# Attention on one core: half of each product with V moved between the next scores and the transposes, and output evictions moved behind maxima and exponentials

## The reference, cut to what matters

```
s = q @ k.T                       # 128 x L scores, L = 256, 512, 640 or 768
p = softmax(s)                    # with exp(sink) in the sum in win0 and win1
out = p @ v                       # 128 x 64
```

## Time and profile before

| | |
|---|---|
| median of 3 runs | 2659.6 us (2650.29 to 2662.57) |
| the profiled execution | 2654.18 us, of which the span of its records is 2652.4 us |
| granted TensorE clock over the span | 0.965 of full speed |
| attention `even` | from about 306 to 518 us of the span |
| attention `win0` | from about 2149 to 2247 us |
| attention `win1` | from about 2499 to 2578 us |

### The profile page before, as it was taken

The page is one execution under the profiler, slowest core; times in us unless marked ns, Lnnn a source line. Parts: engine busy times, 40 slices in busy tenths (PEclk is TensorE's granted clock), DMA queues, the critical chain, the costliest instruction groups (busy, mean ns, idle before and its releaser), DMA issues.

```text
span 2652.4 us, 33704 instructions
## 1 busy us (share of the span) xinstructions
PE 2459.0 (93%) x13758; PEld 1967.3 (74%) x13758; DVE 1545.1 (58%) x2428; ACT 947.9 (36%) x1699; POOL 190.3 (7%) x149
## 2 busy tenths in 40 slices
PE   4998898989999999989998889999989989989997
PEld 2875565678888888868886767877768866858765
DVE  4256578638757576665426578878753256363464
ACT  3355556523222121234233332322344135343352
POOL 0000001002101011100000011101100000000010
PEclk8999899999999999999999999999989989999899
DMA  6233200022332332211120144454321120112301
GB/s 233 80 120 114 84 1 1 9 87 88 100 115 98 118 109 95 99 56 64 64 80 1 43 141 157 164 168 145 127 64 59 63 75 1 48 40 86 109 1 64
DMA packets 65994, 223.61 MB, mean 84 GB/s; under 512 B 7216, under 2 KB 10928, under 8 KB 65072
## 3 DMA queue, kind: packets, MB, share of 16 engines
q1 hardware_dynamic: 63648, 214.65, 24.0%
q10 hardware_dynamic: 2192, 6.82, 0.7%
HBM read 219.34 MB, written 2.10 MB: 83 GB/s over the span
## 4 chain that ended last, share of the span: by engine, by line
PE 82%; DVE 9%; ACT 4%; DMA 3%; POOL 1%; issue 1%; SPq 0%; ACTq 0%; DVEq 0%
PE pair L1084 21%; PE pair L1085 20%; PE pair L1086 20%; PE pair L1251 5%; PE side L1300 3%; PE pair L1287 2%; DMA RAW<-in_w 2%; DVE T L1950 2%; ACT T L1697 1%; PE side L1287 1%; PE pair L1110 1%; DVE ACC L1939 1%; DVE WL L1799 1%; PE pair L763 1%; PE pair L1262 1%
## 5 line engine op out<-in xcount | busy, mean ns | idle before, releaser
L1084 PE MATMUL pair<-HH,WH 128*128 128x512 f32 (+1 forms) x2496 | 887.3, 355 | 44.6 <-DVE HL L1958 36.5
L1085 PE MATMUL pair<-HL,WH 128*128 128x512 f32 (+1 forms) x2496 | 872.7, 350 | 0.0
L1086 PE MATMUL pair<-HH,WL 128*128 128x512 f32 (+1 forms) x2496 | 871.9, 349 | 0.0
L1799 DVE TENSOR_TENSOR WL<-RAW,WH 128x1024 fp32r<-128x1024 f32 (+4 forms) x286 | 314.2, 1099 | 524.3 <-ACT WH L1399 513.8
L1399 ACT CAST WH<-RAW 128x1024 fp32r<-128x1024 f32 (+4 forms) x286 | 271.4, 949 | 889.3 <-DMA RAW<-in_w 887.0
L1084 PEld LDWEIGHTS pair<-HH,WH 128*128 128x128 f32 x2496 | 478.7, 192 | 129.7 <-DVE HL L1958 48.5
L1086 PEld LDWEIGHTS pair<-HH,WL 128*128 128x128 f32 x2496 | 479.4, 192 | 59.8
L1085 PEld LDWEIGHTS pair<-HL,WH 128*128 128x128 f32 x2496 | 480.5, 192 | 58.3 <-issue 1.2
L1939 DVE SCALAR_TENSOR_TENSOR ACC<-MODW,CVF,ACC 128x512 f32<-128x512 f32 x336 | 305.5, 967 | 0.0
L1084 PE MATMUL pair<-DH,WH 128*128 128x512 f32 (+1 forms) x624 | 227.9, 365 | 11.8 <-POOL DL L2311 10.4
L1085 PE MATMUL pair<-DL,WH 128*128 128x512 f32 (+1 forms) x624 | 220.8, 354 | 0.0
(11 more groups left out here) (317 smaller groups left out, 2563.7 us busy)
## 6 DMA issues: line engine op xcount, KB each, us to landing
RAW<-in_w SPq DMA_DIRECT2D x250, 512.0 KB, 3.5
MODW<-in_w SPq DMA_DIRECT2D x96, 512.0 KB, 4.3
RAW<-in_w SPq DMA_DIRECT2D x48, 384.0 KB, 3.0
RAW<-in_w SPq DMA_DIRECT2D x16, 256.0 KB, 2.6
DFL<-in_dft_lat ACTq DMA_DIRECT2D x4, 1024.0 KB, 7.2
X<-in_x SPq DMA_DIRECT2D x1, 3072.0 KB, 15.9
out_x<-X SPq DMA_DIRECT2D x8, 256.0 KB, 2.0
RAW<-in_w SPq DMA_DIRECT2D x8, 192.0 KB, 2.4
```

The costliest lines, as they stand in the source:

```text
L1084: mm(out[0:j.m, c:e], wh[k], a, start=k == 0, stop=False)
L1085: mm(out[0:j.m, c:e], wh[k], b, start=False, stop=False)
L1086: ins = mm(out[0:j.m, c:e], wl[k], a, start=False, stop=k == j.k - 1)
L1799: TT(WL[:, j.n % NRING, 0:c], RAW[:, j.n % NRING, 0:c], WH[:, j.n % NRING, 0:c].bitcast(F32), ALU.subtract).then_inc(*dve.mark("lo", j.n))
```

## The change

In PE's loop the half product `pv` no longer follows `turn(u)`. In iteration u it stands between `scores(u+1)` and `turn(u)`, and its index is one less (half u-3 in place of half u-2). The three halves that are left after the loop are computed there. In ACT's loop the output of a block stands behind the exponentials of the next pair and no longer ahead of the first eviction; in DVE's loop it stands behind the two maxima of the next pair.

```diff
@@ PE @@
                 for u in range(n):
                     if u + 1 < n:
                         scores(u + 1)
+                    if u >= 3:
+                        pv((u - 3) // 2, (u - 3) % 2)
                     turn(u)
-                    if u >= 2:
-                        pv(u // 2 - 1, u % 2)
-                for half in range(2):
-                    pv(n // 2 - 1, half)
+                for i in range(n - 3, n):
+                    pv(i // 2, i % 2)
@@ ACT @@
                 for u in range(n):
-                    if u >= 4 and u % 2 == 0:
-                        out(u // 2 - 2)
                     evict(u, 0, 0)
                     if u + 1 < n:
                         exps(u + 1, 0)
                         exps(u + 1, 1)
+                    if u >= 4 and u % 2 == 0:
+                        out(u // 2 - 2)
                     evict(u, 1, 0)
                     evict(u, 1, 1)
```

## The result

The changed kernel takes 2729.54 us (median of 4 runs, 2726.03 to 2734.86), the kernel before 2654.94 us over the same comparison: a ratio of 1.0273 (95% interval 1.0253 to 1.0294), slower by 74.6 us. The profiled execution took 2732.15 us. (In experiment 9 one execution of six was disturbed as a whole, 4138.74 us at a granted clock of 0.555; its ratio and the median given there leave it out.)

The account below looks back on a forecast made before the run. PE, 100% busy in 768-key GQA, and a chain through the other engines both took 4.57 us a pair. Terms 16.3 + 1.2 + 3.3 + 10.7 + 16.5 + 12.7 = 60.7 us gave 2714.9 or 2720.3, forecast 2717, range 2695 to 2742.

Parts of the forecast that it names:

- The half product comes into the chain at full length: 768-key GQA pairs: the 1.44 us half delays the exponentials, 5.93 us a pair against 4.57, 16.3 us over 12 pairs.
- MLA: First layer's MLA attention: 3.05 us more for six rounds, 21 rounds touched, 10.7 us in all, bounds 6 and 21.
- GQA's small pairs: The 8 GQA pairs of 256 keys: between 0 and 6.7 us more, half taken, 3.3 us.
- The three rounds behind them: Three earlier 768-key GQA pairs that meet a small half: 4.97 us a pair, 0.40 more each, 1.2 us.
- The windows: Halves of one, two and three tiles in `win0` and `win1`: 16.5 us more in the first, 12.7 in the second.
- The clock: GQA stretch with PE busy 77%: no loss, since a row at 76% showed a granted clock of 1.00.
- rival 3: Attention rounds with idle PE lose full clock: up to 2857 us, mild form at window starts 2737; chance 0.06 above 80 more.
- my signs of being wrong: Profile after: an exponential before its round's first eviction, 4.6 us spacing in GQA, or a 0.5 clock in these stretches.
- The outputs: Outputs behind ACT's exponentials and DVE's maxima: nothing or some 0.2 us every second GQA pair, at most 2 us, hidden.
- PE's waits within the transposes: Transposes' waits for evictions (10.4 and 10.3 us) and scaling (4.9): given no gain, bound 25.6 us gained.

Follow-up runs that it names:

- experiment 9: The changed kernel run again without edits, for a second profile and a comparison on the same chip: 2727.1 us, 1.0278.
- experiment 4: Against the changed kernel, ACT's first eviction of each pair moved between the two exponentials of the next pair: 2683.25 us, 1.0096 to the kernel before.
- experiment 5: Against the kernel before, the half product put between the first group of transposes and the other three, outputs as before: 2650.19 us, 0.9983.
- filled kernel: The changed kernel with the fourth transpose group of GQA and window pairs written four, five or ten times: 2723.51 us, 1.0259; run again 2722.09 us, 1.0237.
- experiment 1: Against the changed kernel, the outputs on ACT and DVE put back in their old places, PE's order as changed: 2761.2 us, 1.0387 to the kernel before.
- experiment 2: Against the kernel before, only the outputs moved on ACT and DVE, PE's order as before: 2703.5 us, 1.0166.
- experiment 3: Against the kernel before, the whole change in the first layer's attention only, the windows in the old order: 2698.17 us, 1.0146.
- experiment 6: Against the kernel before, the half product put between the third and fourth groups of transposes: 2648.86 us, 0.9973.

## Why the prediction was right, point by point

- *The half product comes into the chain at full length.* Right, to the hundredth where the chain is regular: 5.92 for 5.93 forecast in 12 rounds, which are 16.2 us for 16.3; 6.02 for 4.58 + 1.44 in the windows. With 0.96 for two tiles I had 5.54 and the profiles show 5.59, so a half of two tiles is 1.0. Experiments 4 and 5 show it from two sides: free the first exponential of the eviction and 46 us come back, of which part may be clock; put the half product behind the first group and nothing of the cost is left (0.9983, against 1.0387 with the outputs in the same places).
- *MLA.* 12.8 for 10.7. The rounds with a large half cost 0.77 (0.79 forecast), those with a small one 0.55 where I had scaled 0.48 from the large: the price of a short group isn't in proportion to its products. Why, no run shows. The three rounds with small pairs cost 1.01, 0.14 and 0.35, 1.5 for the 1.3 taken between 0 and 4.3.
- *GQA's small pairs.* 5.4 for the 3.3 that I put halfway between its bounds, a guess and not a sum; 2.7 of it in a single round, in which the scaling on DVE took 1.82 us beside POOL, and 1.4 in the next, at a granted clock of 0.50 (450 to 454). The three rounds behind them gave 1.8 for 1.2.
- *The windows.* In `win0` the filled kernel is 15.5 above the kernel before, for 16.5 forecast; its clock also rose a round or two earlier (its third round took 2.69, the same one 3.48 before), which hides some 0.9. Taken round by round at full clock, the halves' cost sums to about 16.6. In `win1` the 12.9 for 12.7 is partly luck: two rounds more than in the kernel before ran at full clock at its start (3.0 us gained), and two later ones fell from it (7.29 and 7.39, some 3.7 lost).
- *The clock.* This is the term of the sum that was mis-sized, and where my reading was wrong. I took no loss, since a row before had shown 1.00 at a busy share of 76%, and kept a stay at half clock as the mild form of rival 3. The 12 rounds of GQA with 768 keys did hold 1.00 at 77% busy, and in the first profile the rest of `win0` at 79%. But at the start of a window the clock rose later (`win0` took 13.8 us more than with the filled kernel in the first profile, 3.6 more in the second), and single rounds fell from full clock: 7.29 and 7.39 in `win1` in the first profile, 7.23 in `win0` in the second. In experiments 1 and 2, with other waits in their rounds, it fell regularly, in every fourth round of GQA (0.77 and 0.79), and came back each time. So one row at 76% didn't bear the conclusion that I drew from it. What the Trainium skill says of short idle times in each round ("TensorE: Matmul & The Clock Gate", on a second HAM failure mode) is borne out by those two kernels and by the single rounds, and not by the 12 rounds that held 1.00; I set it aside too fast.
- *What the clock cost.* Of my signs of being wrong, a clock of 0.50 was seen, though in the first rounds of `win0` and not in the stretches that I named. In the first profile `win0` makes 12.8 of the 17.6 us above the forecast. Of the medians' 74.6, the comparisons with the filled kernel put 4 to 11 us down to the clock, for the 13.9 above 60.7; the rest is in MLA and in GQA's small pairs. That a late rise also came with the old order (experiment 3) means that how much of it belongs to the change isn't settled.
- *The outputs.* That their new place is hidden behind the half product was right in the changed kernel (rounds of 5.92 with an output and without), and experiments 2 and 4 show what it costs without that cover.
- *PE's waits within the transposes* were given nothing, rightly: for ACT's evictions they were 10.4 and 10.3 us and are 10.9 and 9.8 in the changed kernel. Experiments 5 and 6 found where a half product does cover them.

What isn't settled: what makes the clock rise at one time or another in the same program. The filled kernel, in two of two profiles, has it up within two or three rounds of `win0`, and at 1.00 from there to the end of that part; how much work that needs isn't shown, and every profile has one to three rounds of 5.5 us, at half clock, at the start of `win1`.

## What to carry to other kernels

An engine at 100% can have a chain through the other engines running beside it at the same period. Then its instructions are not equal: one that the chain passes through can't be delayed, and one that is off the chain belongs behind whatever the chain next waits for. Before moving work, add up both rounds, the engine's own and the chain's, and ask for each new place whether the chain's next release comes before it or after it; one group of transposes further on, with the outputs in the same places, made the difference between 3.9% lost and nothing lost (experiments 1 and 5). And check the granted clock of every stretch before a long round is put down to a wait.

## What the runs showed of the hardware that I had not expected

- In two profiles of the same program TensorE was granted its full clock in `win0` some 15 us after the first exponential of that part in one (about 2208) and some 53 us after it in the other (about 2239), and the execution was 8 us longer. The times of the kernel with idle rounds spread over 20 us, those of the filled one over 9.
- In experiments 1 and 2, regular rounds of GQA at 1.00 had every fourth one at 0.77 or 0.79, with 1.00 again in the next: 7.57 for 5.93, and 8.3 for 6.7.
- A scaling of 128x256 on DVE takes 0.35 us as a rule. One that starts while POOL works on tiles in SBUF ends 0.14 to 0.16 after POOL's instruction does (12 of 12 in the kernels before and after), so its length is a matter of when it starts: 0.39 to 1.51 us in the kernel before, up to 1.82 in the changed one. DVE's maxima and evictions, which read PSUM, aren't lengthened there (0.74 for two and 0.28). The longest one:

```profile
446.64 1.80 POOL L2290 TENSOR_TENSOR HL<-OTF,HH 128x768 fp32r<-128x768 f32 x1
446.78 1.82 DVE L2181 TENSOR_SCALAR T<-T,STAT 128x256 f32<-128x256 f32 x1
...
448.65 0.18 PEld L1287 LDWEIGHTS side<-CONST,T 128*128 128x128 f32 x1 [1.92 <-DVE T L2181]
```

PE's transposes waited 1.92 for it, and that round took 5.05 us where the kernel before has 2.38.
